# The three bodies of an expert item share their beginning and end in TensorE's program, and tail rows are transposed and gathered later

## The reference

```
def moe(h, w_router, b_router, w_gu, b_gu, w_down, b_down):
    ...
    top_val, top_idx = lax.top_k(logits, TOP_K)
    probs = jax.nn.softmax(top_val, axis=-1)
    ...
    gu = lax.ragged_dot(xs, w_gu, group_sizes) + b_gu[e_sorted]
    gate = jnp.minimum(gu[:, :D_FF], SWIGLU_LIMIT)
    up = jnp.clip(gu[:, D_FF:], -SWIGLU_LIMIT, SWIGLU_LIMIT)
    act = gate * jax.nn.sigmoid(SWIGLU_ALPHA * gate) * (up + 1.0)
    out = lax.ragged_dot(act.astype(w_down.dtype), w_down, group_sizes) + b_down[e_sorted]
    out = out * probs.reshape(-1)[order][:, None].astype(out.dtype)
    y = jax.ops.segment_sum(out, tok_sorted, num_segments=n)
```

## Time and profile before

| | |
|---|---|
| median of 3 runs | 2466.28 us (2464.57 to 2467.04) |
| the profiled execution | 2469.84 us, span of its instructions 2468.3 us |
| PE busy | 2211.7 us, 90% of the span |
| DVE, ACT, POOL busy | 65%, 51%, 27% |
| items on PE | from about 828 us to 2376 us |
| granted TensorE clock, mean | 0.928 of full speed |

### The profile page before, as it was taken

The page is one execution under the profiler, slowest core; times in us unless marked ns, Lnnn a source line. Parts: engine busy times, 40 slices in busy tenths (PEclk is TensorE's granted clock), DMA queues, the critical chain, the costliest instruction groups (busy, mean ns, idle before and its releaser), DMA issues. The chain is left out here.

```text
span 2468.3 us, 38942 instructions
## 1 busy us (share of the span) xinstructions
PE 2211.7 (90%) x12114; PEld 1601.7 (65%) x12115; DVE 1605.0 (65%) x2240; ACT 1264.2 (51%) x1662; POOL 664.8 (27%) x936
## 2 busy tenths in 40 slices
PE   6889999999975699999999899999999999999755
PEld 5667777666942467667676657777776777776431
DVE  2344455454224668778786668988797797997447
ACT  1233333333210557557675557767676676775432
POOL 2223332332121313223221123332332233241100
PEclk8999999999576799999999999999999999999875
DMA  9670000000021978788786668989798798997416
GB/s 374 250 243 28 10 31 34 34 32 30 5 67 52 358 270 296 277 298 316 278 332 243 244 224 308 386 314 347 276 389 281 281 371 275 383 365 277 146 31 232
DMA packets 143778, 554.62 MB, mean 225 GB/s; under 512 B 20832, under 2 KB 35437, under 8 KB 109317
## 3 DMA queue, kind: packets, MB, share of 16 engines
q1 hardware_dynamic: 118319, 497.22, 52.2%
q0 software_dynamic: 23680, 51.82, 9.1%
q10 hardware_dynamic: 1694, 4.40, 0.5%
HBM read 512.31 MB, written 41.25 MB: 224 GB/s over the span
## 5 line engine op out<-in xcount | busy, mean ns | idle before, releaser
L1727 DVE TENSOR_TENSOR lo<-raw,hi 128x1024 fp32r<-128x1024 f32 x800 | 933.1, 1219 | 209.9 <-ACT hi L1655 208.5
L1655 ACT ACTIVATE hi<-raw 128x1024 fp32r<-128x1024 f32 x800 | 795.7, 1049 | 152.2 <-PE pg L1600 151.6
L1597 PE MATMUL pg<-hi,xs 128*128 128x512 f32 x1056 | 425.0, 402 | 0.0
L1598 PE MATMUL pg<-lo,xs 128*128 128x512 f32 x1056 | 420.0, 398 | 3.5 <-issue 3.5
L1600 PE MATMUL pg<-hi,xs 128*128 128x512 f32 x1056 | 334.5, 398 | 0.0
L1597 PEld LDWEIGHTS pg<-hi,xs 128*128 128x128 f32 x1056 | 200.8, 190 | 78.2 <-issue 30.3
L1600 PEld LDWEIGHTS pg<-hi,xs 128*128 128x128 f32 x1056 | 200.2, 190 | 48.8
L1598 PEld LDWEIGHTS pg<-lo,xs 128*128 128x128 f32 x1056 | 200.8, 190 | 46.5
L347 PE MATMUL X<-hT,w_in 128*128 128x128 f32 (+1 forms) x1728 | 226.6, 291 | 0.8 <-issue 0.8
L1525 PE MATMUL py<-hi,aT 128*128 128x512 f32 x528 | 220.1, 417 | 5.5 <-ACT aT L1667 5.5
L347 PEld LDWEIGHTS X<-hT,w_in 128*128 128x128 f32 x1728 | 222.1, 210 | 1.2 <-issue 1.2
(11 more groups left out here) (320 smaller groups left out, 2818.7 us busy)
## 6 DMA issues: line engine op xcount, KB each, us to landing
raw<-in_w_gu SPq DMA_DIRECT2D x268, 1024.0 KB, 9.9
raw<-in_w_down SPq DMA_DIRECT2D x132, 1024.0 KB, 9.7
w_out<-in_w_ada SPq DMA_DIRECT2D x10, 2048.0 KB
w_in<-in_w_in SPq DMA_DIRECT2D x5, 2048.0 KB, 18.2
moe_rows<-small SPq DMA_DIRECT2D x9, 512.0 KB, 11.4
x<-in_x_prompt SPq DMA_DIRECT2D x8, 512.0 KB, 3.3
w_in<-in_w_ada SPq DMA_DIRECT2D x2, 2048.0 KB
xr<-in_x_prompt SPq DMA_DIRECT2D x8, 512.0 KB, 3.5
```

Source lines behind the costliest of these rows:

```text
L1597: pe.matmul(pg[u][b][:, :], xs[:, kt, 0, :], wh[:, u, :], start=False, stop=False)
L1598: pe.matmul(pg[u][b][:, :], xs[:, kt, 0, :], wl[:, u, :], start=False, stop=False)
L1655: act.activation(hi[q % RING][:, :, :], grain(q % GRAINS), ACT.Copy).then_inc(s["hi"], 1)
L1727: dve.tensor_tensor(lo[q % RING][:, :, :], grain(q % GRAINS), hi[q % RING][:, :, :].bitcast(F32), ALU.subtract).then_inc(s["lo"], 1)
```

## The change

In PE's program, the bias and the first four grains (`head`, `HEAD = 4`) now stand ahead of the branch on the class, and the last down grains, from the fifth on (`foot`, `FOOT = 4`), stand once behind it. The three bodies keep what lies between. So that the head can be common, the tail rows are transposed behind the first four grains instead of ahead of them. `up_grain`, `down_grain`, `bias` and `down_tail` are the old code as functions. The four semaphore increments that an item without a tail does in place of the tail's work also move behind the head.

On POOL the gather of the tail rows (`gather_tail`) is split off: it now comes behind the copies of the `now` lists, and it alone waits for `xt_ps`. ACT, DVE and SP have the same code as before.

```
-        def per_class(eng, body):
+        def per_class(eng, body, head=None, foot=None):
 
             def choose(i, cls):
+                if head:
+                    head(i)
+                split(i, cls)
+                if foot:
+                    foot(i)
...
             def item(i, tail):
                 pool.wait_ge(s["x_ps"], i * 2 + 2)
-                pool.wait_ge(s["xt_ps"], i + 1)
                 gather(i + 1)
                 pool.wait_ge(s["y_out"], i * 32 + 32)
...
                 pool.wait_ge(s["now"], i + 1)
+                pool.wait_ge(s["xt_ps"], i + 1)
+                pool.sem_inc(s["met"], 1)
+                gather_tail()
                 rotate(i + 1)
...
+            HEAD, FOOT = 4, 4
...
+            def head(i):
+                for q in range(HEAD):
+                    if q < 2:
+                        bias(i, q)
+                    up_grain(i, q)
+
             def item(i, tail):
                 if tail:
                     tail_rows(i, tail)
-                for q, (kt, b) in enumerate(ORDER):
...
+                else:
+                    for name in ("xt_ps", "gt_mm", "aTt_ps", "yt_mm"):
+                        pe.sem_inc(s[name], 1)
+                for q in range(HEAD, GU):
...
-                for kt in range(KT - 2):
+                for kt in range(FOOT):
...
+                pe.wait_ge(s["aT"], i * 2 + 2)
+                if tail:
+                    down_tail(i, FOOT, tail).then_inc(s["yt_mm"], 1)
+
+            def foot(i):
+                for kt in range(FOOT, KT - 2):
+                    down_grain(i, kt)
                 pe.wait_ge(s["lo"], i * GRAINS + GRAINS)
...
-            per_class(pe, item)
+            per_class(pe, item, head, foot)
```

More of the change, by code:

```diff
@@ L1367, in each_item, with split @@
             rounds(eng, lambda i, cls: body(i))
-        def per_class(eng, body):
+        def per_class(eng, body, head=None, foot=None):
             def choose(i, cls):
+                if head:
[3 more added lines that the diff above has]
+                    foot(i)
+            def split(i, cls):
                 with eng.If(cls < 1):
@@ L1459, in gather, with gather_tail @@
                                         bass.IndirectOffsetOnAxis(ap=idx[:, 0:1], axis=0)).then_inc(s["xg"], 16)
+            def gather_tail():
                 pool.indirect_dma_start(xg_t[:, :], None, scratch["h2"][:, :],
@@ L1565, in tail_down, with down_tail, bias, up_grain @@
                 return last
+            def down_tail(i, first, T):
+                for c in range(2):
+                    pe.wait_ge(s[f"raw{KT + first // 2 + c}"], i * 16 + 16)
+                for k in range(4):
+                    last = tail_down(first + k, T)
+                return last
+            HEAD, FOOT = 4, 4
+            def bias(i, b):
+                if b == 0:
+                    pe.wait_ge(s["sel"], i + 1)
+                    pe.wait_ge(s["xlo"], i * 2 + 2)
+                    pe.wait_ge(s["y_t"], i + 1)
+                pe.wait_ge(s["up"], i * 2 + 1 + b)
+                for u in range(2):
+                    pe.matmul(pg[u][b][:, :], sel[:, :], bgu[:, u * FF + b * 512:u * FF + (b + 1) * 512], start=True, stop=False)
+            def up_grain(i, q):
+                kt, b = ORDER[q]
+                pe.wait_ge(s["lo"], i * GRAINS + q + 1)
+                wh, wl = hi[q % RING], lo[q % RING]
+                for u in range(2):
+                    pe.matmul(pg[u][b][:, :], xs[:, kt, 0, :], wh[:, u, :], start=False, stop=False)
+                    pe.matmul(pg[u][b][:, :], xs[:, kt, 0, :], wl[:, u, :], start=False, stop=False)
+                for u in range(2):
+                    last = pe.matmul(pg[u][b][:, :], xs[:, kt, 1, :], wh[:, u, :], start=False, stop=(kt == KT - 1))
+                last.then_inc(s["used"], 1)
+            def down_grain(i, kt):
+                pe.wait_ge(s["lo"], i * GRAINS + GU + kt + 1)
+                for n in range(2):
+                    down_hi(kt, n)
+                if kt % 4 == 0:
+                    pe.wait_ge(s["alo"], i * 2 + kt // 4 + 1)
+                for n in range(2):
+                    last = down_lo(kt, n)
+                last.then_inc(s["used"], 1)
+            def head(i):
[3 more added lines that the diff above has]
+                    up_grain(i, q)
             def item(i, tail):
@@ L1569, in item @@
                     tail_rows(i, tail)
-                for q, (kt, b) in enumerate(ORDER):
[L1571 to L1584, removed]
+                else:
+                    for name in ("xt_ps", "gt_mm", "aTt_ps", "yt_mm"):
+                        pe.sem_inc(s[name], 1)
+                for q in range(HEAD, GU):
+                    if tail and q in TAILED:
+                        pe.wait_ge(s["lo"], i * GRAINS + q + 1)
                     if tail and q == min(TAILED):
@@ L1614, in item @@
                         transpose_rows(i + 1, 1)
[L1615 to L1633, removed]
+                    if tail and kt == 0:
+                        pe.wait_ge(s["aT_t"], i + 1)
+                        down_tail(i, 0, tail)
+                    down_grain(i, kt)
[4 more added lines that the diff above has]
+                for kt in range(FOOT, KT - 2):
+                    down_grain(i, kt)
                 pe.wait_ge(s["lo"], i * GRAINS + GRAINS)
```

## The result

| | before | after |
|---|---|---|
| median | 2465.43 us (2462.38 to 2467.04, 4 runs) | 2427.12 us (2425.58 to 2432.20, 4 runs) |
| profiled execution, span | 2469.84 us, 2468.3 us | 2426.97 us, 2425.4 us |
| items on PE in it | 828.0 to 2376.6: 1548.6 us | 821.7 to 2333.5: 1511.8 us |

The account below looks back on a forecast made before the run. PE's own work bounds the kernel, with stalls where item code isn't on the core. Stalls -36.6 and first use -1.0 sum to -37.6 us: 2432.2 us profiled, 2428.7 us as median; range 2423 to 2442 us.

Parts of the forecast that it names:

- forecast A: PE's item loop: after the change all code blocks stay once brought, no stall behind item 1; 2428.7 us, chance 0.80.
- its signs: Instruction queue: 27 packets, none behind item 1; no PE branch there over 1 us; items 11, 13, 32 at 50, 37.6, 61 us.
- 8 blocks kept against 9: PE's item loop lay in 8 blocks of 256 instructions, 9 with the one brought ahead; only 8 are kept.
- quiet stretch: 368 us with eight items of classes 0 and 32 in turn and one packet, using 8 blocks, all kept.
- the one ahead: The block following the one PE enters, brought ahead; it adds one to the blocks the loop needs.
- the two packets that stalled nothing: Instruction queue packets of 1640 to 1690 us, taken to show that the following block is brought ahead.
- Stalls that go: PE in items 10 to 13 and 31 to 32: 16.38 and 20.24 us too long, together 36.6 us won.
- First use: Items 0 and 1, blocks brought once, jump to the foot misses: -1 us; bounds 4 us less to 4 us more.
- Cost 0: branches, transposes, ACT, POOL: Moved jumps, tail transposes in mid-item, ACT's copy into `xs_t` 1.1 us later, POOL's gather 3 us later: 0 each.
- B, some stalls stay: PE's loop: another block gets in, a few of six stalls remain at 3.5 to 7 us each; 2446 us, chance 0.11.
- C, nothing gained: PE's loop: blocks are kept by distance of jumps, not loop size, so the stalls return; 2466 us, chance 0.03.
- D, slower: PE's foot is replaced, misses at each of 19 class changes cost 66 us; 2494 us, chance 0.06.

Follow-up runs that it names:

- the foot alone: Kernel before with only the last four down grains shared; transposes, gathers and order of work old: 2427.95 us, ratio 0.9859.
- 96 increments: Kernel before with 96 semaphore increments that nobody waits for, run once on PE ahead of the item loop: 2426.72 us, ratio 0.9855.
- the order alone: Changed kernel with head and foot written out in each of the three bodies again, PE's code as long as before: 2459.26 us, ratio 0.9982.
- 200 increments: Kernel before with 200 idle semaphore increments run once on PE ahead of the item loop: 2461.95 us, ratio 0.9992.
- the unused code: Changed kernel with 288 never-run increments ahead of PE's body for 64, behind a never-true condition: 2457.70 us, ratio 0.9963.
- blocks of 36: Changed kernel with the outer loop over blocks of 36 items instead of 24: 2418.09 us, ratio 0.9800; run again, 2420.37 us, ratio 0.9809.
- the three kernels with increments: Kernel before with idle increments ahead of the loop: 96, 2426.72 us; 200, 2461.95 us; 96 and outer blocks of 36 items, 2419.95 us.

## Why the prediction was right

*The mechanism, forecast A.* Right in all its signs: 27 packets, none behind 930 us, no branch over 1 us behind item 1, and the items 11, 13 and 32 as long as their like. The count of 8 blocks kept against 9 was taken from one stall and one quiet stretch. It has since held for five other layouts of the code: 8 blocks with the one ahead in the foot alone and with 96 increments, and no stalls; 9 in the order alone, with 200 increments and with the unused code, and the stalls. What these runs separate is a loop of 7 blocks from a loop of 8. That the block brought ahead takes one of 8 places like any other is argued from the quiet stretch and from the two packets that stalled nothing.

*Stalls that go, -36.6 us.* Items 10 to 13 now take 1501.08 - 1289.33 = 211.75 us, and 31 and 32 to the last matmul 2333.13 - 2209.57 = 123.56 us: 15.7 and 19.5 us less. Each of the two stretches now holds the transposes of its first item, 0.70 us, which stood ahead of its bias before. With that, 16.4 and 20.2 us, 36.7 in all: the term is right to 0.1 us. The experiment with 96 increments, which moves no transposes, gives 211.1 and 122.9 us directly, against 211.10 and 122.85 forecast.

*First use, -1 us.* No gain shows here, but the term is too small for these runs to settle. From the first bias of item 0 to that of item 3 it was 100.4 + 39.9 = 140.3 us, and is 102.1 + 37.55 + 0.70 for item 3's transposes = 140.4 us: +0.1. Three more profiles with the same PE code in these items (the changed kernel again and both with blocks of 36) give 139.1, 139.6 and 139.1 us counted in the same way, and the three kernels with increments, whose items have the old code, 139.6, 138.9 and 138.9: profiles of like code differ by more than the term. Both jumps to the foot missed, as said. In this profile they showed 3.80 and 4.11 us, 0.7 us more than the 7.19 us of the earlier trace rows, and in the other three 6.8 to 7.5 us together. Of the two branches PE's queued work hid 2.4 and 1.3 us (6.21 - 3.80, 5.37 - 4.11). In item 1 the jump comes right behind the tail's down matmuls, which take 1.93 / 32 = 0.06 us each, so a queue full of them is soon empty; that is my reading, no run tested it.

*Cost 0: branches, transposes, ACT, POOL.* Right. The 32-row items take 50.45 to 50.5 us (item 1 and item 23, 50.68, apart), and the items 3 to 9 327.9 us in both kernels. Item 24 is 0.85 us longer than before, which the 0.2 us of the prediction didn't allow; with item 23 and its transposes it is 93.1 us in both. ACT's copy waited 1.11 us (forecast 1.1 us later), and its idle time fell to 2.10 us (about 2).

*The sum.* -37.6 us forecast. The items give 1511.8 - 1548.6 = -36.8 us, the medians -38.3 us, 2427.12 us against 2428.7. The profiled pair differs by 42.9 us, because item 0 begins 6.3 us earlier in one of them, after code that is the same in both; over the profiles of all kernels this start scatters from 821 to 829 us. A sum that takes its whole difference from one pair of profiles would have been wrong by that.

*The rivals.* B, some stalls stay: none did, though the fit is exact. C, nothing gained because what is kept goes by the distance of jumps: refuted. Two kernels with the very jumps of the one before, 96 increments apart from it, and 104 from each other, stand at 2426.7 and 2462.0 us. With it falls, for TensorE, the rule of two kept blocks (the Trainium skill, "Runtime: NRT & Kernel Launch", section "Instruction fetch mechanics"): by it no layout of this loop could be free of packets for 1400 us, as these are. But the prediction read that section only in part. The same section of the Trainium skill gives TensorE's instruction memory as 128 KiB or 2048 instructions, refilled in blocks of 256, and that makes 8 blocks. The runs agree with this figure, 8 kept. D, slower because the foot is replaced: it isn't. When 9 blocks are needed again, with the unused code, the time is still 7.4 us under the kernel before, not above it.

*What the prediction could have said and didn't.* Its own count, 9 blocks needed and 8 kept, with a loop of 6.3 blocks behind an edge, already implied that the foot alone or a shift of the loop's beginning would do. It priced the whole change and so left open which part earned the gain. It also said that every place where PE stands still is marked "issue", and so passed over the 4 us at item 24, which an edit of one line removes.

## What to carry over

When an engine stands still with "issue" as its only reason, look at the branches of its sequencer and at the packets of the instruction queue, and count the code of the loop in packets. If it misses by one block, shift it before you restructure it: 96 harmless instructions ahead of the loop won here what a rewrite did. And make any such gain robust: 104 more instructions at the same place took it away again.

## What the runs showed of the hardware

What is replaced is not simply the oldest block. In the kernel before, item 0 jumps to the loop's end at 864.4 us and misses (a branch of 6.36 us, its packet at 868.4 us). Item 1 jumps to the same place at 921.4 us and misses again (4.65 us), though only three packets (874.0, 886.3 and 913.7 us) came in between. I compared the packets of each kernel, item by item, with a model that keeps 8 blocks and chooses what to replace by a binary tree of last-used bits, with one block brought ahead. It gives the measured totals of the first seven kernels: 59 before, 27 after, 59, 28, 28, 60, 59. With replacement by age alone it gives two too few, and misses that item 1 fetched the end of the loop again. The model is fitted and argued, not shown by a run of its own; it wasn't tried with other numbers of blocks.

A jump whose code isn't there takes 3.3 to 3.8 us at L1361, and 3.7 to 7.2 us at L1372, L1375 and their successors. In the kernel before, two packets start within each of the three longest behind item 1 (6.35, 5.92 and 7.14 us), one within each of those at L1361. Behind such a stall the granted clock is lower for a while (0.66 at item 11), and item 11 took 52.27 us instead of 50.45: 1.8 us that no idle time shows.
